# Linear-attention scan: levels paired by s and t+1, without a diagonal pass

## Chip, core and metric

One core of a Trainium2 chip runs one launch of the kernel. The metric is the device time of that launch in microseconds. The kernel before takes 2003.21 us in the median of three runs (2000.13 to 2006.03). The engines are named PE (matmuls), PEld (its weight loads), DVE (vector), ACT (scalar), POOL (GpSimd) and SP (which queues most transfers).

## The reference

The program is a stack of mixer and feed-forward parts on 512 tokens of width 1024, in fp32. The change lies in its first part, a linear attention with 8 heads of 128 features. Cut to that:

```
q = silu(q) * 128 ** -0.5
forget = lower_bound + (1 - lower_bound) * sigmoid(f)
k = 1 - forget
# per head, per chunk: cum = cumsum(log forget)
decay[t, s] = exp(cum[t] - cum[s])            # for s <= t, else 0; per feature
scores[t, s] = sum over features of q[t] * k[s] * decay[t, s]
o = scores @ v + (q * exp(cum)) @ state
state = exp(cum[last]) * state + (k * exp(cum[last] - cum)).T @ v
o = rms_norm(o, out_norm) * silu(g)           # then @ w_out
```

The decay of a pair (t, s) is the product of the forget values from s+1 to t, a vector over features, so it has to be put into q and k before the matmul over features.

## The kernel before, in words

All matmuls against weights are split in three: weights and activations are each a high and a low part of fp32r, and high x high, high x low and low x high are added (L329, L332, L333, three 128x512 matmuls a tile of 128x128 weights). ACT makes the high part of a chunk of 8 weight tiles (L1208), DVE the low one (L1887), both some chunks ahead.

**A head of the scan.** The 512 tokens are four blocks of 128, and q, k, the forget values (`ff`) lie with features on partitions and tokens along the row. Within a block the pairs (t, s) are sorted into the diagonal (s = t) and 7 levels. At level lv, spans of b = 2^lv tokens are taken in pairs: s lies in the first span, t in the second. The kernel walks the levels from 0 to 6. Before a level's scores, q in the second spans and k in the first ones have been multiplied step by step by the products of forget values that lie between (DVE: `qt`, L2040; POOL: `kt`, L2726), and POOL halves the row of forget products (`ft`, L2733, into `fb`). Each level is one pass of four matmuls, one a block (L441, `scores`; an fp32 matmul shows as two records in the trace), and one masked copy of the 128x512 result into `sc` (DVE, `pick`, L2022). The masks of the diagonal and the 7 levels come from `masks()` by a transfer at the start.

The diagonal's pass uses q itself (`a.q`, two buffers) before any product; the levels use `qa = q * ff` (L2009), one buffer. So `qa` waits until the output matmuls of the head before have read it. The passes use banks 3 and 4 in turn.

After the last level PE transposes k (L469), makes the states (L476) and the outputs (L487 with `sc`, L490 with `qa` and the state S); ACT takes the squares and the root (L1318, L1322), DVE scales (`og`, L2069), PE transposes `og` (L500), DVE applies gain and gate (L2075), and ACT and DVE split it into `ohi` (L1327) and `olo` (L2078), the operands of the output projection.

**The order.** Each engine runs its own program, written out by hand; semaphores named by head and level tie them (`sc_mm`: a pass is done; `qt`, `kt`, `ft`: the products; `cp`: the masked copy). `HG_TILES` says how many weight tiles of the next head's projections PE, ACT and DVE take after each step of a head's scan: none before the first pass, none between the diagonal and level 0, three behind level 0, two behind each later level. The last head's scan has the first tiles of the output projection there. An engine's instructions run in program order, so an instruction that waits holds all that stand behind it.

Of the kernel before, what the change touches and what calls it, by code (L numbers as in the profile page):

```python
# [9 lines left out]
I32 = mybir.dt.int32  # L10
# [5 lines left out]
T = 512  # L16
# [94 lines left out]
def memory(nc, ctx):  # L111
# [32 lines left out]
    with ExitStack() as ph:  # L144
        p = lambda name, shape, dt=F: sbt(ph, name, shape, dt)
        a = m.hg = Names()
        a.v = p("v", [128, 4, D])
        a.ohi = p("ohi", [128, KD, T], FR)
        a.olo = p("olo", [128, KD, T], FR)
        a.tq = p("tq", [128, 2, T])  # L150
        a.th = p("th", [128, 2, T])
        a.q = p("q", [128, 2, T])
        a.ff = p("ff", [128, 2, T])
        a.kk = p("kk", [128, 2, T])
        a.sg = p("sg", [128, 2, T])
        a.qa = p("qa", [128, T])
        a.fb = p("fb", [128, T])
        a.sc = p("sc", [128, 4, 128])
        a.kt = p("kt", [128, 3, 128])
        a.S = p("S", [128, 3, 128])  # L160
        a.og = p("og", [128, 2, T])
        a.mask = p("mask", [128, LV + 1, 128])
        a.ssq = p("ssq", [128, 2, 4])
        a.rch = p("rch", [128, 4])

# [111 lines left out]


HG_V_BANKS = [[0, 1, 2, 3], [4, 5, 6, 0]]
HG_TILES = [0, 0, 3, 2, 2, 2, 2, 2, 2, 2, 1, 1, 1, 3, 0, 1]  # L280
SWA_LEAD = 3
SWA_TILES = [4, 0, 1, 0, 0, 0, 1, 2, 0]
SWA_BEGUN = [0] * 6 + [1] * 7 + [0] + [2] * 7
# [36 lines left out]
def tensor_program(e, m, s):  # L320
# [82 lines left out]

    def hgrn():
        a = m.hg
        kk, qs, sc, S, v, qa = a.kk, a.q, a.sc, a.S, a.v, a.qa
        ready0 = operands_ready("n0")
        for g in range(2):
            for k in range(KD):
# [24 lines left out]
        def scan(h):  # L434
            z = h % 2
            hc = slice(128 * h, 128 * h + 128)

            def scores(level, b, qx):
                for c in range(4):
                    cs = slice(128 * c, 128 * c + 128)  # L440
                    op = e.matmul(B[b][:, cs], kk[:, z, cs], qx[:, cs], start=True, stop=True)  # L441
                op.then_inc(*s.sc_mm.tick(h, level))

            yield
            q.wait_ge(*s.made_v.at("k", h))
            if h:
                q.wait_ge(*s.made_a.at("kt", h - 1))
            else:
                q.wait_ge(*s.taken_a.at("v", 0, 3))
            scores(0, 3, qs[:, z, :])  # L450
            yield
            for lv in range(LV):
                if lv == 0:
                    q.wait_ge(*s.made_v.at("qa", h))
                    if h:
                        q.wait_ge(*s.made_v.at("S", h - 1, 2))
                    else:
                        q.wait_ge(*s.taken_a.at("v", 1, 0))
                else:
                    q.wait_ge(*s.qt.at(h, lv - 1))  # L460
                    q.wait_ge(*s.kt.at(h, lv - 1))
                    q.wait_ge(*s.cp.at(h, lv - 1))
                scores(lv + 1, 4 - lv % 2, qa)
                yield
            q.wait_ge(*s.kt.at(h, LV - 1))
            q.wait_ge(*s.cp.at(h, 6))
# [6 lines left out]
            q.wait_ge(*s.cp.at(h, 7))  # L473
            for c in range(3):
                cs = slice(128 * c, 128 * c + 128)
                op = e.matmul(B[4][:, cs], a.kt[:, c, :], v[:, c, hc], start=True, stop=True)  # L476
            op.then_inc(*s.valued.tick("S", h))
            yield
            bo = B[5 + z]
            if h > 1:  # L480
                q.wait_ge(*s.taken_v.at("o", h - 2))
            else:
                q.wait_ge(*s.taken_a.at("v", 1, 1 + h))
            q.wait_ge(*s.qt.at(h, LV - 1))
            for c in range(4):
                cs = slice(128 * c, 128 * c + 128)
                op = e.matmul(bo[:, cs], sc[:, c, :], v[:, c, hc], start=True, stop=c == 0)  # L487
                if c:
                    q.wait_ge(*s.made_v.at("S", h, c - 1))
                    op = e.matmul(bo[:, cs], qa[:, cs], S[:, c - 1, :], start=False, stop=True)  # L490
# [708 lines left out]
def scalar_program(e, m, s, A, chunks):  # L1199
# [69 lines left out]
    def hgrn():  # L1269
# [26 lines left out]
        def scan(h):  # L1296
            z = h % 2
            yield
            yield
# [580 lines left out]
def vector_program(e, m, s, chunks):  # L1880
# [94 lines left out]

    def hgrn():
        a = m.hg
        kk, ff, qs, sc, S, qa, th, tq, fb = a.kk, a.ff, a.q, a.sc, a.S, a.qa, a.th, a.tq, a.fb
        first_rows()
        root("n0", m.rc)  # L1980
        tables()
# [4 lines left out]
        def proj(h):  # L1986
# [19 lines left out]
            q.wait_ge(*s.made_v.at("q", h))  # L2006
            if h:
                q.wait_ge(*s.filled.at("o", h - 1))
            e.tensor_tensor(qa[:, :], qs[:, z, :], ff[:, z, :], MUL).then_inc(*s.made_v.tick("qa", h))  # L2009
            yield from w.steps(KD - 3)  # L2010

        def scan(h):
            z = h % 2

            def pick(level, b):
                q.wait_ge(*s.sc_mm.at(h, level))
                if level:
                    q.wait_ge(*s.cp.at(h, level - 1))
# [3 lines left out]
                e.copy_predicated(sc[:, :, :], a.mask[:, level, :].bitcast(I32).unsqueeze(1).to_broadcast((128, 4, 128)),  # L2022
                                  B[b].rearrange("p (c t) -> p c t", c=4)).then_inc(*s.cp.tick(h, level))

            yield
            pick(0, 3)
            yield
            fsrc = ff[:, z, :]
            for lv in range(LV):
                b = 1 << lv  # L2030
                n = T // (2 * b)
                fs = fsrc[:, 0:2 * n].rearrange("p (n a) -> p n a", a=2)
                qv = qa[:, :].rearrange("p (n a b) -> p n a b", a=2, b=b)
                q.wait_ge(*s.sc_mm.at(h, lv + 1))
                if lv:
                    q.wait_ge(*s.qt.at(h, lv - 1))
                    q.wait_ge(*s.ft.at(h, lv - 1))
                else:
                    q.wait_ge(*s.made_v.at("qa", h))
# [10 lines left out]
                o0 = 0 if lv % 2 == 0 else 256  # L2050
                fsrc = fb[:, o0:o0 + n]
                yield
            yield
            q.wait_ge(*s.valued.at("S", h))
# [655 lines left out]
def pool_program(e, m, s):  # L2710
    q = Waits(e)

    def hgrn(h):
# [3 lines left out]
        for lv in range(LV):  # L2717
# [4 lines left out]
            q.wait_ge(*s.sc_mm.at(h, lv + 1))  # L2722
            if lv:
                q.wait_ge(*s.kt.at(h, lv - 1))
                q.wait_ge(*s.ft.at(h, lv - 1))
            e.tensor_tensor(kv[:, :, 0, :], kv[:, :, 0, :], fs[:, :, 1:2].to_broadcast((128, n, b)),  # L2726
                            MUL).then_inc(*s.kt.tick(h, lv))
            fdst = a.fb[:, 256 * (lv % 2):256 * (lv % 2) + n]
            if h and lv == 0:
                q.wait_ge(*s.made_v.at("S", h - 1, 2))  # L2730
            if lv:
                q.wait_ge(*s.qt.at(h, lv - 1))
            e.tensor_tensor(fdst.unsqueeze(2), fs[:, :, 0:1], fs[:, :, 1:2], MUL).then_inc(*s.ft.tick(h, lv))  # L2733
            fsrc = fdst

    def sum_of_squares(site, i, width=T):
# [366 lines left out]
```

## Time and profile before

| what | value |
|---|---|
| median of three runs | 2003.21 us |
| lowest, highest | 2000.13, 2006.03 us |
| profiled execution | 2006.37 us |
| its span, first to last instruction | 2004.5 us |
| mean granted PE clock | 0.988 |
| PE, DVE, ACT, POOL busy | 97%, 69%, 42%, 11% |
| chain that ended last | PE 80%, DVE 12%, ACT 5%, issue 3% |

The profiled execution's own time is its span and some 2 us around it. Shares are means over stages with different limits; the scan takes about 220 of the 2004.5 us. Idle time of an engine counts only where another engine waits for it.

### The profile page before, as it was taken

How to read it: one execution, taken by the hardware profiler on the slowest of the kernel's cores; microseconds unless marked ns; L12 is line 12 of the kernel's file. 1: busy time of each engine (PE TensorE's matmuls, PEld its weight loads, DVE VectorE, ACT ScalarE, POOL GpSimd, SP SyncE). 2: the span in 40 equal slices, each digit the busy share in tenths (PEclk: the TensorE clock that was granted, in tenths of full speed). 3: DMA queues.
4: the chain of work that ended last, by engine and by line, in shares of the span. 5: the costliest groups of instructions: out<-in, count | busy, mean ns of one | idle time of the engine just before them, and what ended most of it. 6: DMA issues, size and time to landing. Idle time of an engine off the chain costs nothing.

```text
span 2004.5 us, 24575 instructions
## 1 busy us (share of the span) xinstructions
PE 1946.8 (97%) x9790; PEld 1632.7 (81%) x9790; DVE 1377.7 (69%) x1978; ACT 836.0 (42%) x1326; POOL 228.7 (11%) x233
## 2 busy tenths in 40 slices
PE   7999999999999999999999999999999999999997
PEld 6888887788888889888888888778888778888786
DVE  5477766997789578857755874555655477787774
ACT  5233334441233356644423443454444444454442
POOL 2133221003201230010000001000000101001011
PEclk9999999999999999999999999999999999999998
DMA  5211112335544431134343432311101323232321
GB/s 184 74 57 64 53 64 95 142 126 200 184 154 145 136 124 43 45 103 148 136 168 116 157 104 87 105 63 43 43 33 32 126 74 118 99 137 84 130 95 53
DMA packets 60818, 207.73 MB, mean 104 GB/s; under 512 B 6816, under 2 KB 7264, under 8 KB 59552
## 3 DMA queue, kind: packets, MB, share of 16 engines
q1 hardware_dynamic: 53152, 192.53, 28.3%
q10 hardware_dynamic: 7552, 13.64, 1.9%
q8 instruction: 77, 1.26, 0.3%
q14 instruction: 37, 0.30, 0.1%
HBM read 195.65 MB, written 10.49 MB: 103 GB/s over the span
## 4 chain that ended last, share of the span: by engine, by line
PE 80%; DVE 12%; ACT 5%; issue 3%; POOL 1%; DMA 1%; ACTq 0%; DVEq 0%; SPq 0%
PE PS L329 21%; PE PS L333 20%; PE PS L332 20%; PE PS L441 3%; DVE wlo L1887 2%; PE PS L945 2%; PE PS L336 1%; PE PS L339 1%; PE PS L340 1%; PE PS L737 1%; ACT whi L1208 1%; PE PS L934 1%; DVE col_f L2108 1%; PE PS L549 1%; PE PS L718 1%
## 5 line engine op out<-in xcount | busy, mean ns | idle before, releaser
L329 PE MATMUL PS<-nhi,whi 128*128 128x512 f32 x1456 | 589.7, 405 | 15.5 <-DVE wlo L1887 3.5
L333 PE MATMUL PS<-nhi,wlo 128*128 128x512 f32 x1456 | 572.4, 393 | 0.0
L332 PE MATMUL PS<-nlo,whi 128*128 128x512 f32 x1456 | 571.4, 392 | 0.0
L1887 DVE TENSOR_TENSOR wlo<-raw,whi 128x1024 fp32r<-128x1024 f32 x290 | 367.4, 1276 | 176.7 <-ACT whi L1208 175.5
L1208 ACT ACTIVATE whi<-raw 128x1024 fp32r<-128x1024 f32 x290 | 302.1, 1052 | 182.5 <-PE PS L329 112.4
L329 PEld LDWEIGHTS PS<-nhi,whi 128*128 128x128 f32 x1456 | 276.6, 190 | 77.4 <-issue 9.7
L333 PEld LDWEIGHTS PS<-nhi,wlo 128*128 128x128 f32 x1456 | 275.7, 189 | 60.1
L332 PEld LDWEIGHTS PS<-nlo,whi 128*128 128x128 f32 x1456 | 276.7, 190 | 52.2 <-issue 1.0
L2741 POOL TENSOR_TENSOR diag<-diag,sqb 128x512 f32<-128x512 f32 (+1 forms) x56 | 73.0, 1304 | 758.5 <-ACT sqb L1217 675.8
L329 PE MATMUL PS<-hh_f,whi 128*128 128x512 f32 x352 | 137.8, 392 | 0.0
L333 PE MATMUL PS<-hh_f,wlo 128*128 128x512 f32 x352 | 137.7, 391 | 0.0
L332 PE MATMUL PS<-hl_f,whi 128*128 128x512 f32 x352 | 137.5, 391 | 0.0
L2757 POOL TENSOR_TENSOR sd_f<-ab_f 128x512 f32<-128x512 f32 x32 | 55.3, 1745 | 271.6 <-DVE ab_f L2196 271.0
L2108 DVE SCALAR_TENSOR_TENSOR col_f<-aw_f,scv,col_f 128x1024 f32<-128x1024 f32 x63 | 85.0, 1359 | 0.0
L329 PEld LDWEIGHTS PS<-hh_f,whi 128*128 128x128 f32 x352 | 66.5, 189 | 13.9
L332 PEld LDWEIGHTS PS<-hl_f,whi 128*128 128x128 f32 x352 | 66.5, 189 | 13.8
L333 PEld LDWEIGHTS PS<-hh_f,wlo 128*128 128x128 f32 x352 | 66.3, 188 | 14.0
L1431 ACT ACTIVATE t_f<-gp_f,par 128x512 f32<-128x512 f32 x44 | 35.9, 816 | 94.3 <-DVE gp_f L2213 94.3
L1673 ACT ACTIVATE pt_m<-PS 128x768 f32<-128x768 f32 x32 | 26.0, 812 | 110.9 <-PE PS L934 110.9
L1931 DVE TENSOR_TENSOR hT<-hT,PS 128x512 f32<-128x512 f32 x48 | 32.7, 681 | 49.7 <-PE PS L333 49.6
L1907 DVE SCALAR_TENSOR_TENSOR nlo<-hT,par,nhi 128x512 fp32r<-128x512 f32 x32 | 38.9, 1222 | 37.4 <-ACT nhi L1230 37.4
L1217 ACT ACTIVATE sqb<-hT 128x512 f32<-128x512 f32 x42 | 26.5, 630 | 90.4 <-DVE hT L1931 57.9
(365 smaller groups left out, 3363.4 us busy)
## 6 DMA issues: line engine op xcount, KB each, us to landing
raw<-in_stream SPq DMA_DIRECT2D x290, 512.0 KB, 3.5
aw_f<-in_ada SPq DMA_DIRECT2D x48, 512.0 KB, 4.5
rows<-sd_f ACTq DMA_DIRECT2D x32, 256.0 KB, 2.3
rows_h<-rows SPq DMA_DIRECT2D x8, 1024.0 KB, 6.1
wd_f<-in_decay ACTq DMA_DIRECT2D x16, 256.0 KB, 2.9
hT<-in_xT SPq DMA_DIRECT2D x8, 256.0 KB, 7.5
out<-hT SPq DMA_DIRECT2D x8, 256.0 KB, 2.0
wd_f<-in_filt_out ACTq DMA_DIRECT2D x8, 128.0 KB, 2.9
```

The costliest lines, as they stand in the source:

```text
L329: op = e.matmul(out, hi, xh, start=first, stop=False)
L332: e.matmul(out, hi, xl, start=False, stop=False)
L333: return e.matmul(out, lo, xh, start=False, stop=last)
L441: op = e.matmul(B[b][:, cs], kk[:, z, cs], qx[:, cs], start=True, stop=True)
L945: op = e.matmul(B[6][:, 128 * blk:128 * blk + 128], a.v[:, t, 128 * h:128 * h + 128], a.pt[:, i, 128 * t:128 * t + 128], start=t == 0, sto ...
L1208: e.activation(m.whi[:, c % HL, :], m.raw[:, c % RAW, :], ACT.Copy).then_inc(*s.w_hi.tick(c))
L1431: e.activation(a.t[:, 0, z, :], a.gp[:, z, 2:T + 2], ACT.Identity, bias=pc(cb, f), scale=pc(cw, 44 + f)).then_inc(*s.made_a.tick("c0", lay ...
L1887: e.tensor_tensor(m.wlo[:, c % HL, :], m.raw[:, c % RAW, :], m.whi[:, c % HL, :].bitcast(F), SUB).then_inc(*s.w_lo.tick(c))
L1907: e.scalar_tensor_tensor(m.nlo[:, k, :], m.hT[:, k, :], gain, m.nhi[:, k, :].bitcast(F), MUL, SUB).then_inc(*s.nlo.tick(site, k))
L2108: e.scalar_tensor_tensor(col[:, v, :], aw[:, n % AW[layer], :], m.scv[:, 2, k, v:v + 1], col[:, v, :], MUL, ADD).then_inc(*s.made_v.tick(" ...
L2741: e.tensor_tensor(acc, acc, m.sqb[:, i % 2 if site != "n4" else 0, 0:width], ADD).then_inc(*s.acc.tick(site, i))
L2757: e.tensor_tensor(a.sd[:, x, :], a.ab[:, 0, :], a.ab[:, 1, :], SUB if x else ADD).then_inc(*s.made_p.tick("sd", n, i, x))
```

## The change

Levels are found from s and u = t + 1 in place of s and t. A pair with s = t then has s and u in neighbouring spans of some level, so the diagonal needs no pass. Pairs whose u is 128, the last token of a block, are in no level by this rule; the last token's q is kept in two extra columns of each block. Column HG_U + 128 is its running product, multiplied by forget products at level 5 and 6, and column HG_U + 129 the raw value, the diagonal of the last token.

So q lies in a row of four blocks of 160 columns, with u = 0 at column 15; `qa` and its product q * ff are gone, and the level products work on q in place. The last level scores 81 columns in place of 128, and two plain copies of parts of the block take the place of its masked copy. There are two masks fewer, and one step of the scan fewer in the order of PE, ACT and DVE, with its 0 in `HG_TILES`. POOL makes the forget product before the key product at level 5 alone. The writing of q waits for the output matmuls of two heads before.

```diff
-        a.q = p("q", [128, 2, T])
+        a.q = p("q", [128, 2, 4, 160])
-        a.qa = p("qa", [128, T])
-        a.mask = p("mask", [128, LV + 1, 128])
+        a.mask = p("mask", [128, LV - 1, 128])
...
-HG_TILES = [0, 0, 3, 2, 2, 2, 2, 2, 2, 2, 1, 1, 1, 3, 0, 1]
+HG_TILES = [0, 3, 2, 2, 2, 2, 2, 2, 2, 1, 1, 1, 3, 0, 1]
+HG_U = 15
+HG_LAST = 49
...
@@ tensor_program, scan @@
-            def scores(level, b, qx):
+            def scores(lv, b):
+                first = HG_LAST if lv == LV - 1 else 1
+                n = 130 - HG_LAST if lv == LV - 1 else 128
                 for c in range(4):
-                    op = e.matmul(B[b][:, cs], kk[:, z, cs], qx[:, cs], start=True, stop=True)
+                    op = e.matmul(B[b][:, 128 * c:128 * c + n], kk[:, z, 128 * c:128 * c + 128],
+                                  qs[:, z, c, HG_U + first:HG_U + first + n], start=True, stop=True)
...
-            q.wait_ge(*s.made_v.at("k", h))
-            if h:
-                q.wait_ge(*s.made_a.at("kt", h - 1))
-            else:
-                q.wait_ge(*s.taken_a.at("v", 0, 3))
-            scores(0, 3, qs[:, z, :])
-            yield
...
@@ vector_program, proj @@
-            e.scalar_tensor_tensor(qs[:, z, :], th[:, 0, :], 1.0, tq[:, 0, :], ADD, MUL).then_inc(*s.made_v.tick("q", h))
+            if h > 1:
+                q.wait_ge(*s.filled.at("o", h - 2))
+            last = lambda x: in_blocks(x)[:, :, 127:128]
+            e.scalar_tensor_tensor(qs[:, z, :, HG_U + 129:HG_U + 130], last(th[:, 0, :]), 1.0, last(tq[:, 0, :]), ADD,
+                                   MUL).then_inc(*s.made_v.tick("raw", h))
+            e.scalar_tensor_tensor(qs[:, z, :, HG_U + 1:HG_U + 129], in_blocks(th[:, 0, :]), 1.0, in_blocks(tq[:, 0, :]), ADD,
+                                   MUL).then_inc(*s.made_v.tick("q", h))
...
-            if h:
-                q.wait_ge(*s.filled.at("o", h - 1))
-            e.tensor_tensor(qa[:, :], qs[:, z, :], ff[:, z, :], MUL).then_inc(*s.made_v.tick("qa", h))
...
@@ vector_program, scan @@
+                if lv < LV - 1:
+                    op = e.copy_predicated(sc[:, :, :], a.mask[:, lv, :].bitcast(I32).unsqueeze(1).to_broadcast((128, 4, 128)), got)
+                else:
+                    e.tensor_copy(sc[0:64, :, 63:128], got[0:64, :, 64 - HG_LAST:129 - HG_LAST])
+                    op = e.tensor_copy(sc[64:128, :, 127:128], got[64:128, :, 129 - HG_LAST:130 - HG_LAST])
...
-                e.tensor_tensor(qv[:, :, 1, :], qv[:, :, 1, :], fs[:, :, 0:1].to_broadcast((128, n, b)),
-                                MUL).then_inc(*s.qt.tick(h, lv))
-                pick(lv + 1, 4 - lv % 2)
+                if lv < LV - 1:
+                    qv = qs[:, z, :, HG_U:HG_U + 128].rearrange("p c (n a b) -> p c n a b", a=2, b=b)[:, :, :, 1, :]
+                    op = e.tensor_tensor(qv, qv, fs[:, :, :, 0:1].to_broadcast((128, 4, n // 4, b)), MUL)
+                else:
+                    qv = qs[:, z, :, HG_U + 64:HG_U + 129]
+                    op = e.tensor_tensor(qv, qv, fs[:, :, 0, 0:1].to_broadcast((128, 4, 65)), MUL)
+                op.then_inc(*s.qt.tick(*((h, "row", lv) if lv == LV - 2 else (h, lv))))
...
+                if lv == LV - 2:
+                    x = qs[:, z, :, HG_U + 128:HG_U + 129]
+                    q.wait_ge(*s.ft.at(h, lv))
+                    e.tensor_tensor(x, x, in_blocks(fsrc)[:, :, 1:2], MUL).then_inc(*s.qt.tick(h, lv))
+                pick(lv, 4 - lv % 2)
...
@@ pool_program, hgrn @@
+            if lv == LV - 2:
+                forgets()
+                keys()
+            else:
+                keys()
+                forgets()
...
@@ masks @@
-    out = [s == t]
-    for lv in range(LV):
+    u = t + 1
+    out = []
+    for lv in range(LV - 1):
         b = 1 << lv
-        out.append((s // (2 * b) == t // (2 * b)) & (s // b % 2 == 0) & (t // b % 2 == 1))
+        out.append((s // (2 * b) == u // (2 * b)) & (s // b % 2 == 0) & (u // b % 2 == 1))
```

## Rows read from the trace of the kernel before

**Rows 1.** The page's busy times: busy us, share of the span, instructions.

```profile
PE 1946.8 (97%) x9790; PEld 1632.7 (81%) x9790; DVE 1377.7 (69%) x1978; ACT 836.0 (42%) x1326; POOL 228.7 (11%) x233
```

**Rows 2.** Windows, one head: PE, PEld, DVE, ACT, POOL busy (records), clock, DMA share, GB/s.

```profile
157.00:185.00 28.00, 27.56 (x166) 23.59 (x167) 20.23 (x34) 9.88 (x19) 8.67 (x14) 1.00 0.18 57
```

**Rows 3.** Groups by form, 75 to 297 us: busy us, mean ns, idle before.

```profile
L441 PE MATMUL PS<-qa,kk 128*128 128x128 f32 x448 | 60.1, 277 | 0.8
...
L2022 DVE COPY_PREDICATED sc<-mask,PS 128x512 f32<-128x512 int32 x64 | 47.7, 745 | 2.2 <-PE PS L441 2.2
...
L441 PE MATMUL PS<-q,kk 128*128 128x128 f32 x64 | 8.4, 274 | 0.0
...
L2009 DVE TENSOR_TENSOR qa<-q,ff 128x512 f32<-128x512 f32 x7 | 4.8, 693 | 1.4 <-PE PS L490 1.4
```

**Rows 4.** Chain of waits in order of time: start us, us, what.

```profile
158.31 1.78 PE PS L441 x16
...
162.18 0.89 PE PS L441 x8
...
454.06 3.46 PE PS L549 x32
```

**Rows 5.** Groups by form, 90 to 620 us: small operations on DVE.

```profile
L2055 DVE COPY S<-PS 128x128 f32<-128x128 f32 x8 | 2.3, 292 | 6.2 <-PE PS L476 6.2
...
L2065 DVE RECIPROCAL rch<-sd 128x4 f32<-128x4 f32 x8 | 1.4, 179 | 18.6 <-ACT sd L1322 18.6
```

**Rows 6.** Timeline: start of the fourth head's scan, DVE and POOL.

```profile
159.53 0.69 DVE L2078 TENSOR_TENSOR olo<-og,ohi 128x512 fp32r<-128x512 f32 x1 [0.69 <-ACT ohi L1327]
...
160.18 0.86 POOL L2726 TENSOR_TENSOR kk<-kk,ff 128x256 f32<-128x256 f32 x1 [11.92 <-PE PS L441]
...
160.80 0.52 DVE L2040 TENSOR_TENSOR qa<-qa,ff 128x256 f32<-128x256 f32 x1
...
160.99 0.80 POOL L2733 TENSOR_TENSOR fb<-ff 128x256 f32<-128x256 f32 x1
```

**Rows 7.** Timeline: the first head's level 0 on DVE.

```profile
77.00 0.43 DVE L2040 TENSOR_TENSOR qa<-qa,ff 128x256 f32<-128x256 f32 x1 [0.17 <-PE PS L441]
```

**Rows 8.** Timeline: levels 1 to 4 of the fourth head.

```profile
162.01 1.05 PE L441 MATMUL PS<-qa,kk 128*128 128x128 f32 x8
...
163.10 0.43 DVE L2040 TENSOR_TENSOR qa<-qa,fb 128x256 f32<-128x256 f32 x1 [0.55 <-PE PS L441]
...
163.15 1.00 POOL L2726 TENSOR_TENSOR kk<-kk,fb 128x256 f32<-128x256 f32 x1 [1.36 <-PE PS L441]
...
164.29 1.09 PE L441 MATMUL PS<-qa,kk 128*128 128x128 f32 x8
...
166.62 1.05 PE L441 MATMUL PS<-qa,kk 128*128 128x128 f32 x8
...
167.10 1.21 DVE L1887 TENSOR_TENSOR wlo<-raw,whi 128x1024 fp32r<-128x1024 f32 x1
...
167.75 1.06 POOL L2726 TENSOR_TENSOR kk<-kk,fb 128x256 f32<-128x256 f32 x1 [1.12 <-PE PS L441]
...
168.23 0.86 DVE L2040 TENSOR_TENSOR qa<-qa,fb 128x256 f32<-128x256 f32 x1
...
169.15 1.16 PE L441 MATMUL PS<-qa,kk 128*128 128x128 f32 x8
...
171.54 1.05 PE L441 MATMUL PS<-qa,kk 128*128 128x128 f32 x8
```

**Rows 9.** Timeline behind the scan: a POOL and a DVE operation together.

```profile
304.49 1.30 POOL L2741 TENSOR_TENSOR diag<-diag,sqb 128x512 f32<-128x512 f32 x1 [17.63 <-ACT sqb L1217]
...
305.06 1.28 DVE L1907 SCALAR_TENSOR_TENSOR nlo<-hT,par,nhi 128x512 fp32r<-128x512 f32 x1 [1.31 <-ACT nhi L1230]
```

**Rows 10.** Timeline: the fourth head's last level.

```profile
173.82 1.05 PE L441 MATMUL PS<-qa,kk 128*128 128x128 f32 x8
...
174.91 0.43 DVE L2040 TENSOR_TENSOR qa<-qa,fb 128x256 f32<-128x256 f32 x1 [0.62 <-PE PS L441]
```

More of the change, by code:

```diff
@@ L405, in hgrn @@
         a = m.hg
-        kk, qs, sc, S, v, qa = a.kk, a.q, a.sc, a.S, a.v, a.qa
+        kk, qs, sc, S, v = a.kk, a.q, a.sc, a.S, a.v
         ready0 = operands_ready("n0")
@@ L436, in scan @@
             hc = slice(128 * h, 128 * h + 128)
-            def scores(level, b, qx):
+            def scores(lv, b):
+                first = HG_LAST if lv == LV - 1 else 1
+                n = 130 - HG_LAST if lv == LV - 1 else 128
                 for c in range(4):
-                    cs = slice(128 * c, 128 * c + 128)
-                    op = e.matmul(B[b][:, cs], kk[:, z, cs], qx[:, cs], start=True, stop=True)
-                op.then_inc(*s.sc_mm.tick(h, level))
-            yield
-            q.wait_ge(*s.made_v.at("k", h))
-            if h:
-                q.wait_ge(*s.made_a.at("kt", h - 1))
-            else:
-                q.wait_ge(*s.taken_a.at("v", 0, 3))
-            scores(0, 3, qs[:, z, :])
+                    op = e.matmul(B[b][:, 128 * c:128 * c + n], kk[:, z, 128 * c:128 * c + 128],
+                                  qs[:, z, c, HG_U + first:HG_U + first + n], start=True, stop=True)
+                op.then_inc(*s.sc_mm.tick(h, lv))
             yield
@@ L453, in scan @@
                 if lv == 0:
-                    q.wait_ge(*s.made_v.at("qa", h))
+                    q.wait_ge(*s.made_v.at("q", h))
+                    q.wait_ge(*s.made_v.at("k", h))
                     if h:
@@ L461, in scan @@
                     q.wait_ge(*s.kt.at(h, lv - 1))
-                    q.wait_ge(*s.cp.at(h, lv - 1))
-                scores(lv + 1, 4 - lv % 2, qa)
+                    if lv > 1:
+                        q.wait_ge(*s.cp.at(h, lv - 2))
+                    elif h:
+                        q.wait_ge(*s.made_a.at("kt", h - 1))
+                    else:
+                        q.wait_ge(*s.taken_a.at("v", 0, 3))
+                scores(lv, 4 - lv % 2)
                 yield
             q.wait_ge(*s.kt.at(h, LV - 1))
-            q.wait_ge(*s.cp.at(h, 6))
+            q.wait_ge(*s.cp.at(h, LV - 2))
             for c in range(3):
@@ L472, in scan @@
             q.wait_ge(*s.made_a.at("kt", h))
-            q.wait_ge(*s.cp.at(h, 7))
+            q.wait_ge(*s.cp.at(h, LV - 1))
             for c in range(3):
@@ L489, in scan @@
                     q.wait_ge(*s.made_v.at("S", h, c - 1))
-                    op = e.matmul(bo[:, cs], qa[:, cs], S[:, c - 1, :], start=False, stop=True)
+                    op = e.matmul(bo[:, cs], qs[:, z, c, HG_U + 1:HG_U + 129], S[:, c - 1, :], start=False, stop=True)
             op.then_inc(*s.filled.tick("o", h))
@@ L1298, in scan @@
             yield
-            yield
             for lv in range(LV):
@@ L1977, in hgrn @@
         a = m.hg
-        kk, ff, qs, sc, S, qa, th, tq, fb = a.kk, a.ff, a.q, a.sc, a.S, a.qa, a.th, a.tq, a.fb
+        kk, ff, qs, sc, S, th, tq, fb = a.kk, a.ff, a.q, a.sc, a.S, a.th, a.tq, a.fb
         first_rows()
@@ L2005, in proj @@
             e.tensor_scalar(kk[:, z, :], ff[:, z, :], -1.0, 1.0, MUL, ADD).then_inc(*s.made_v.tick("k", h))
-            q.wait_ge(*s.made_v.at("q", h))
-            if h:
-                q.wait_ge(*s.filled.at("o", h - 1))
-            e.tensor_tensor(qa[:, :], qs[:, z, :], ff[:, z, :], MUL).then_inc(*s.made_v.tick("qa", h))
             yield from w.steps(KD - 3)
@@ L2013, in scan, with pick @@
             z = h % 2
[L2015 to L2018, printed above, removed]
+            def pick(lv, b):
+                got = in_blocks(B[b])
+                q.wait_ge(*s.sc_mm.at(h, lv))
+                if lv:
+                    q.wait_ge(*s.cp.at(h, lv - 1))
                 else:
@@ L2021, in pick @@
                     q.wait_ge(*s.setup_v.at("sc"))
[L2022 to L2026, printed above, removed]
+                if lv < LV - 1:
[3 more added lines that the diff above has]
+                    op = e.tensor_copy(sc[64:128, :, 127:128], got[64:128, :, 129 - HG_LAST:130 - HG_LAST])
+                op.then_inc(*s.cp.tick(h, lv))
             yield
@@ L2031, in scan @@
                 n = T // (2 * b)
-                fs = fsrc[:, 0:2 * n].rearrange("p (n a) -> p n a", a=2)
-                qv = qa[:, :].rearrange("p (n a b) -> p n a b", a=2, b=b)
-                q.wait_ge(*s.sc_mm.at(h, lv + 1))
+                fs = fsrc[:, 0:2 * n].rearrange("p (c n a) -> p c n a", c=4, a=2)
+                q.wait_ge(*s.sc_mm.at(h, lv))
                 if lv:
@@ L2038, in scan @@
                 else:
-                    q.wait_ge(*s.made_v.at("qa", h))
-                e.tensor_tensor(qv[:, :, 1, :], qv[:, :, 1, :], fs[:, :, 0:1].to_broadcast((128, n, b)),
-                                MUL).then_inc(*s.qt.tick(h, lv))
-                pick(lv + 1, 4 - lv % 2)
+                    q.wait_ge(*s.made_v.at("q", h))
+                if lv < LV - 1:
[5 more added lines that the diff above has]
+                op.then_inc(*s.qt.tick(*((h, "row", lv) if lv == LV - 2 else (h, lv))))
+                o0 = 0 if lv % 2 == 0 else 256
+                fsrc = fb[:, o0:o0 + n]
+                if lv == LV - 2:
[3 more added lines that the diff above has]
+                pick(lv, 4 - lv % 2)
                 if lv == 0:
@@ L2049, in scan @@
                                            MUL).then_inc(*s.made_v.tick("sg", h))
-                o0 = 0 if lv % 2 == 0 else 256
-                fsrc = fb[:, o0:o0 + n]
                 yield
@@ L2721, in hgrn, with keys, forgets @@
             kv = kx.rearrange("p (n a b) -> p n a b", a=2, b=b)
[L2722 to L2727, printed above, removed]
-            fdst = a.fb[:, 256 * (lv % 2):256 * (lv % 2) + n]
[L2729 to L2733, printed above, removed]
+            fdst = a.fb[:, 256 * (lv % 2):256 * (lv % 2) + n]
+            def keys():
+                q.wait_ge(*s.sc_mm.at(h, lv))
+                if lv:
+                    q.wait_ge(*s.kt.at(h, lv - 1))
+                    q.wait_ge(*s.ft.at(h, lv - 1))
+                e.tensor_tensor(kv[:, :, 0, :], kv[:, :, 0, :], fs[:, :, 1:2].to_broadcast((128, n, b)),
+                                MUL).then_inc(*s.kt.tick(h, lv))
+            def forgets():
+                if h and lv == 0:
+                    q.wait_ge(*s.made_v.at("S", h - 1, 2))
+                if lv:
+                    q.wait_ge(*s.qt.at(h, lv - 1))
+                    q.wait_ge(*s.ft.at(h, lv - 1))
+                e.tensor_tensor(fdst.unsqueeze(2), fs[:, :, 0:1], fs[:, :, 1:2], MUL).then_inc(*s.ft.tick(h, lv))
+            if lv == LV - 2:
+                forgets()
+                keys()
+            else:
+                keys()
+                forgets()
             fsrc = fdst
```

## Prediction

> **What bounds the kernel now.** I read the page's table of busy times first: PE is busy 97% of the span [rows 1]. Then the stage that the change touches, the eight heads of the scan (about 75 to 297 us), by windows: in the 28 us of one head PE is busy 27.6 us at a granted clock of 1.00, DVE 20.2, POOL 8.7 and the DMA engines 0.18 of the time [rows 2]. So PE sets the pace here, and work taken off DVE alone is worth nothing, unless PE was waiting for it. The groups by form price what goes and what stays [rows 3], the chain of waits gives PE's own pace [rows 4], and the timelines of one head show which operand comes last before each scoring pass [rows 6 to 8]. The head shown is the fourth; the ones after it repeat it.
>
> **PE: what is removed.** The diagonal pass is four fp32 matmuls, 8 records a head, 64 in all [rows 3]. In the chain the two adjoining passes take 1.78 us for 16 records and one pass 0.89 us for 8, so 0.111 us a record [rows 4]. Nothing else runs between them. The pass is worth 0.89 us a head, 8 x 0.89 = 7.1 us if nothing new comes last.
>
> The last level now scores 81 columns in place of 128. Nearest row: 32 records of one column each take 3.46 us, 0.108 us a record [rows 4], nearly the pace of 128 columns. That bounds the gain at 0.003 x 64 = 0.2 us; I take nothing. The Trainium skill (TensorE: Matmul & The Clock Gate, Back-to-back issue gap) gives columns/2.4 + 2.5 ns for an isolated matmul, by which a record of two such passes would fall by about 0.04 us and the 64 records by 2.5 us; the same section says that the formula leaves out the weight load, and the one-column row agrees with that.
>
> **DVE: what is removed and added, a head.** Gone: one masked copy (0.75) and the product q*f (0.69) [rows 3]. The last masked copy becomes two plain copies, of 64 x 260 and 64 x 4. A 128 x 128 copy from PSUM takes 0.29 us and a 128 x 512 masked copy 0.75 [rows 3, 5]; I take 0.43 for the first, and 0.18, as for a 128 x 4 reciprocal [rows 5], for the second, 0.61 together (at most 0.93 by the masked copy). Two operations on 128 x 4 come in, the raw last column and its product: 0.18 each, between nothing and 0.29 [rows 5]. Sum: 2.19 us gone, 0.97 added. DVE has idle time in the head, so this counts only where PE waits for DVE. The products on q now walk four blocks of 160 with the same number of elements; I take the same 0.43 to 0.52 us [rows 6, 8] and no cost, and keep +0.3 us as the upper bound (the data part again), nothing as the lower.
>
> **The start of a head: where a new wait arises.** Today two PE passes stand before the first products, so POOL begins its key product at 160.18, when DVE has just ended the low half of the previous head's output (olo, 159.53 for 0.69) [rows 6]. After the change the first pass is done at 160.09 - 0.89 = 159.20 [rows 4] and POOL starts at about 159.29, before DVE's olo. Both read two SBUF operands. What the trace shows when a POOL operation of that kind is under way and DVE starts such a one: DVE's ends 0.28 us (256 columns) or 0.55 us (512) after POOL's end, however early it began. So the level-3 product, 168.23 for 0.86 beside POOL's 167.75 to 168.81, ends 0.28 after it [rows 8]; the level-0 product, 160.80 for 0.52, ends 0.28 after POOL's 161.04 [rows 6]; a 512-column one at 305.06 takes 1.28 and ends 0.55 after POOL's 305.79 [rows 9]. Whoever waited longer comes next: at 168.31 POOL, waiting behind DVE's weight split, goes ahead of DVE's next product; at 161.04 the waiting DVE product goes ahead of POOL's next. The Trainium skill (SBUF — State Buffer, Who interferes with whom) states this as an exclusive lock on a shared port pair for a DVE instruction with two SBUF inputs against GpSimd; by that rule, the trace agrees.
>
> With these rows the start of the fourth head becomes:
> POOL keys 159.29 to 160.15 (0.86 alone [rows 6]).
> DVE olo from 159.53, held until 160.15, then 0.55: 160.70.
> POOL's forget product, there since 160.10, is next: its 0.47 after a release (today 161.32 to 161.79 [rows 6]): 161.17.
> DVE's level-0 product, there since 160.62: 161.17 + 0.28 = 161.45.
> PE wants the next pass at 162.01 - 0.89 = 161.12 [rows 8]. The product is 0.33 us late.
>
> What lateness costs: level passes that nothing delays start 2.28 us apart (162.01 to 164.29). From 166.62 to 171.54 two steps take 4.92 in place of 4.56, a loss of 0.36, where the level-3 product ended at 169.09, 0.19 after the due 168.90 [rows 8]. So a loss is lateness + 0.17, and 0.33 late costs 0.50 us. This holds for the seven heads with an olo before them. In the first head no olo stands before them, DVE is idle until the pass is done, and its product takes 0.43 [rows 7]: full 0.89.
>
> **Behind it.** The level-1 pass then starts at 161.51 and ends at about 162.67; DVE comes free of g's scaling just then. POOL's level-1 keys end at 163.76 whether DVE's product goes first (162.71 to 163.14, then 0.62 as today [rows 8]) or the DVE product follows (163.80); the pass is due at 161.51 + 2.28 + 0.11 = 163.90. Today the keys end at 164.15 against 164.29 [rows 8]: the same 0.14. Nothing more is lost there, and 0.1 at most. The wait at level 3 (0.36 us) hangs on the weight split behind the level-2 pass, moves with PE and stays. So does the wait for the output's norm at the head's end.
>
> Level 5: POOL makes the forget product first. It needs only level 4's, and POOL waits over a microsecond for each pass (1.36 us before 163.15 [rows 8]), so this fills idle time. DVE's product for the last column then meets POOL's keys and ends right behind them, at about 173.6 against a pass due at 173.82 [rows 10]. Cost nothing; if its 0.18 became 0.5, 0.1 a head. The masked copy and the q of the next head slip by 0.5 us; the level-6 product slips from 174.91 [rows 10] to about 175.6 and ends near 175.9, and is wanted only by the output matmuls, three steps later. The weight split behind it slips with it by some 0.4 us; its chunk is first used more than a chunk's matmuls later. The wait added before q is written, on the output of two heads before, ended a head earlier. Of transfers only the mask block changes, a quarter smaller, and no PE wait hangs on it.
>
> **Sum.** 8 x 0.89 = 7.1; 7 x 0.50 = 3.5 given back; 3.6 us gained. Against the profiled execution, 2006.4 us with a span of 2004.5, that is 2002.8; against the median of the runs, 2003.2, it is 1999.6 us, 0.18% less.
>
> **Rivals.**
> A. The port is not in the way, or DVE keeps it from olo to the product next to it: the product is done by 160.8 to 161.0, before 161.12. The full 7.1 us: 1996.1 us. For it: DVE takes back-to-back instructions with no gap. Against: at 168.31 DVE did lose the port between two of its own. Chance 0.20.
> B. My mechanism, with the block-wise product views, the extra column and the level-1 race each costing some 0.1 us: levels 0 and 3 pass all of it on, together about 0.27 us a head, 2.1 us: 2001.7 us. Chance 0.19.
> C. Slower. The products over four blocks of 160 run at half speed, +0.30 us each. Levels 0 and 3 lose it whole (0.60). POOL's keys wait behind the product: level 1 has 0.14 to spare and loses 0.16 + 0.17, level 2 has 0.25 and loses 0.22, levels 4 and 5 have 0.28 and lose 0.19 each. 1.53 a head, 12.2 in all, less 3.6: 2011.8 us. It turns the sign from about +0.2 us a product, where 0.45 us a head is lost. For it: no row shows DVE on such a view. Against: the products at span 1 and span 2 both take 0.43 undisturbed [rows 7, 8], whatever the step between their elements. Chance 0.07.
> The forecast itself: 0.54.
>
> **Numbers.** A measurement of this kernel can tell about 0.3%, 6.0 us (three runs lie from 2000.1 to 2006.0). The gain of 3.6 us is inside. Faster by over 0.3%: nearly all of A and a tenth of the forecast, 0.24. Slower: C and a little, 0.08. Within: 0.68. The range reaches to A's 1996.1 and a little below, and above B to where nothing is gained: 1995.5 to 2003.5; the forecast's own is 1998 to 2001.5.
>
> **What would show it.** The scoring group has 448 records, not 512; the head's period falls from 27.7 to about 27.3 us from the second head on, and the first by 0.9. Olo takes about 1.2 us in place of 0.69 in seven heads; the level-0 product about 0.8 in place of 0.52; and PE has a new wait for that product before the level-1 pass, seven times. The last-level pass keeps 0.11 us a record. If olo still takes 0.69, A is right; if the products take 0.7 us with POOL idle, C is. It would be wrong, too, if POOL's first keys started later than 159.3, or if a stage behind the scan lost or won time of its own.

## Result and the profile after

The changed kernel takes 1999.02 us in the median of ten runs (1996.57 to 2003.74); the kernel before, in ten, 2005.16 us (2000.13 to 2006.03). The ratio is 0.9977, 95% interval 0.9966 to 0.9988: 4.6 us less (2.4 to 6.8). The two medians lie 6.1 us apart and the two means 4.4 us (2003.7 and 1999.2): of the ten times of the kernel before, three lie at 2000.1 to 2000.5 and seven at 2003.2 to 2006.0, so its median moves easily. The forecast was 3.6 us less and 1999.6 us.

The page of the changed kernel:

```profile
span 1997.5 us, 24456 instructions
...
PE 1938.4 (97%) x9726; PEld 1622.5 (81%) x9726; DVE 1376.4 (69%) x1986; ACT 836.1 (42%) x1326; POOL 231.2 (12%) x233
```

PE has 9726 records, 64 fewer than in [rows 1]. The same 28 us of the fourth head, by windows (the columns as in [rows 2]):

```profile
155.00:183.00 28.00, 27.31 (x160) 23.02 (x161) 20.60 (x35) 9.88 (x19) 9.01 (x14) 1.00 0.19 57
```

The 28 us hold a little more than one head, so for DVE whole heads are the better measure: over the seven from the first to the last transposes of the scaled output it is busy 136.5 us, and in the kernel before 136.4. The work taken off it comes back as four small operations and as time that others spend held. The groups by form show where (busy us, mean ns, idle before):

```profile
L443 PE MATMUL PS<-q,kk 128*128 128x128 f32 x384 | 52.4, 279 | 2.4 <-DVE q L2047 1.5
...
L443 PE MATMUL PS<-q,kk 128*128 128x81 f32 x64 | 8.1, 269 | 0.0
...
L2752 POOL TENSOR_TENSOR fb<-ff 128x256 f32<-128x256 f32 x8 | 8.1, 1006 | 0.0
...
L2092 DVE TENSOR_TENSOR olo<-og,ohi 128x512 fp32r<-128x512 f32 x7 | 8.0, 1149 | 4.9 <-ACT ohi L1328 4.9
...
L2047 DVE TENSOR_TENSOR q<-q,ff 128x256 f32<-128x256 f32 x8 | 6.2, 780 | 2.8 <-PE PS L443 2.8
```

The diagonal's pass is gone (384 + 64 records, where [rows 3] had 448 + 64). Olo (L2092) has a mean of 1.15 us and the level-0 product (L2047 on `ff`) 0.78. Of the new operations the copies from PSUM take 0.41 and 0.17 us, the last level's product 0.43, the raw column 0.15, the last column's product 0.58. The start of the fourth head on the timeline:

```profile
156.21 1.05 PE L443 MATMUL PS<-q,kk 128*128 128x128 f32 x8
...
157.34 0.86 POOL L2743 TENSOR_TENSOR kk<-kk,ff 128x256 f32<-128x256 f32 x1 [11.08 <-PE PS L443]
...
157.59 1.16 DVE L2092 TENSOR_TENSOR olo<-og,ohi 128x512 fp32r<-128x512 f32 x1 [0.70 <-ACT ohi L1328]
...
158.16 1.06 POOL L2752 TENSOR_TENSOR fb<-ff 128x256 f32<-128x256 f32 x1
...
158.67 0.83 DVE L2047 TENSOR_TENSOR q<-q,ff 128x256 f32<-128x256 f32 x1
...
159.56 1.16 PE L443 MATMUL PS<-q,kk 128*128 128x128 f32 x8 [0.21 <-DVE q L2047]
...
160.80 1.00 POOL L2743 TENSOR_TENSOR kk<-kk,fb 128x256 f32<-128x256 f32 x1 [1.58 <-PE PS L443]
...
161.94 1.09 PE L443 MATMUL PS<-q,kk 128*128 128x128 f32 x8
```

The reader should follow the ends. POOL's keys end at 158.20. Olo, under way since 157.59, ends at 158.75, 0.55 later. POOL's forget product, there since 158.16, ends at 159.22, 0.47 later. DVE's level-0 product, there since 158.67, ends at 159.50, 0.28 later. PE was due for the next pass at 159.18, 2.97 us after the first (in the kernel before they are 3.86 apart, 158.15 and 162.01, with the 0.89 us of the removed pass in between), and begins it at 159.56. On the chain of waits this stretch, which was PE's alone in the kernel before [rows 4], now reads:

```profile
157.59 1.16 DVE olo L2092
158.75 0.77 DVE q L2047
...
159.56 1.16 PE PS L443 x8
```

And among the waits of the stage (us, times, longest) stands one that was not there, seven of the fifteen in the first row (the other eight are level 3's) and all of the last:

```profile
PEld PS L443 <- DVE q L2047: 8.8, 15, 0.6
...
PE PS L443 <- DVE q L2047: 1.5, 7, 0.2
```

**Period of a head.** The transposes of the scaled output (L500, in the changed kernel L502) mark each head. The table takes the first and the last of the eight from each timeline, and a seventh of their distance. These periods repeat within 0.06 us from head to head, where whole runs of one kernel differ by 5 us and more.

| kernel | first, last transposes (us) | period | ratio to before, 95% |
|---|---|---|---|
| before | 101.52, 295.58 | 27.72 | |
| changed | 100.39, 291.59 | 27.31 | 0.9977 (0.9966 to 0.9988) |
| e1_olo_late | 101.56, 289.28 | 26.82 | 0.9964 (0.9952 to 0.9977) |
| e2_before_olo_late | 100.54, 294.52 | 27.71 | 0.9996 (0.9985 to 1.0007) |
| e3_olo_one_sbuf | 100.84, 288.94 | 26.87 | 0.9955 (0.9941 to 0.9968) |
| e4_last_128 | 100.13, 291.34 | 27.32 | 0.9980 (0.9971 to 0.9989) |
| e5_keys_first | 101.35, 294.21 | 27.55 | 0.9993 (0.9984 to 1.0002) |
| e6_gate_early | 99.82, 288.32 | 26.93 | 0.9966 (0.9952 to 0.9979) |
| e7_olo_late_gate_early | 99.68, 284.72 | 26.43 | 0.9948 (0.9935 to 0.9962) |
| e8_norm_cover | 100.00, 281.23 | 25.89 | 0.9926 (0.9912 to 0.9940) |
| e9_before_three_moves | 101.31, 288.61 | 26.76 | 0.9960 (0.9946 to 0.9973) |
| e10_all_again | 100.52, 281.60 | 25.87 | 0.9925 (0.9911 to 0.9938) |

In the first head the way from the first pass to the transposes falls from 26.51 us (75.01 to 101.52) to 25.61 (74.78 to 100.39), by 0.90. The scan as a whole, first pass to last transposes, falls from 220.57 to 216.81 us, by 3.76.

### The profile page after: what moved, and what is told of

Same layout as the page of the kernel before. It is cut to its first block, busy times and chain, and to the rows that moved or that the text cites. A ratio compares the mean times of both kernels' runs of the same rounds, so it can differ in the third digit from the quotient of the medians.

```text
span 1997.5 us, 24456 instructions
## 1 busy us (share of the span) xinstructions
PE 1938.4 (97%) x9726; PEld 1622.5 (81%) x9726; DVE 1376.4 (69%) x1986; ACT 836.1 (42%) x1326; POOL 231.2 (12%) x233
## 4 chain that ended last, share of the span: by engine, by line
PE 78%; DVE 13%; ACT 5%; issue 3%; POOL 1%; DMA 0%; ACTq 0%; DVEq 0%; SPq 0%
PE PS L330 20%; PE PS L334 20%; PE PS L333 20%; DVE wlo L1888 3%; PE PS L443 2%; PE PS L947 2%; ACT whi L1210 1%; PE PS L337 1%; PE PS L341 1%; PE PS L340 1%; PE PS L739 1%; PE PS L936 1%; DVE col_f L2122 1%; DVE q L2047 1%; PE PS L551 1%
## 5 line engine op out<-in xcount | busy, mean ns | idle before, releaser
L443 PEld LDWEIGHTS PS<-q,kk 128*128 128x128 f32 x448 | 56.6, 191 | 13.3 <-DVE q L2047 8.8
```

The source lines that it names most:

```text
L443: op = e.matmul(B[b][:, 128 * c:128 * c + n], kk[:, z, 128 * c:128 * c + 128], qs[:, z, c, HG_U + first:HG_U + first + n], start=True, sto ...
```

## The experiments

The theory: a removed pass is worth 0.89 us; in seven heads olo, which reads two SBUF operands, now starts behind POOL's first key product, is held by it, and so makes the level-0 product too late for PE. Each kernel has the change unless said otherwise.

**1. Olo behind the work of level 0.**

```diff
+        def low_part(h):
+            q.wait_ge(*s.hid_hi.at("o", h))
+            e.tensor_tensor(a.olo[:, h, :], ...).then_inc(*s.hid_lo.tick("o", h))
...
@@ level 0, behind the scaling of g @@
+                    if h:
+                        low_part(h - 1)
...
-            q.wait_ge(*s.hid_hi.at("o", h))
-            e.tensor_tensor(a.olo[:, h, :], ...).then_inc(*s.hid_lo.tick("o", h))
+            if h == KD - 1:
+                low_part(h)
```

> The changed kernel, but DVE makes the low half of the previous head's output (olo) behind level 0's product, masked copy and scaling of g, no longer before them; only the order on DVE changes. Theory (olo and POOL's first key product want the same port, and the level-0 product comes out 0.3 us late for PE): olo back to 0.69 us, the level-0 product starts right behind the first pass and takes 0.43 us, no PE wait before the level-1 pass, 0.5 us less a head in the seven later heads, so the scan is 3.3 to 3.5 us shorter than in the changed kernel and the time 7 to 8 us below the kernel before. Rival 1 (PE waits for something else there, for instance POOL's first keys): the wait before the level-1 pass stays, time as the changed kernel. Rival 2 (the gain of a removed pass never was 0.89 us a head): no wait, but the heads stay at 27.3 us.

The timeline of the same head:

```profile
156.37 1.05 PE L443 MATMUL PS<-q,kk 128*128 128x128 f32 x8
...
157.46 0.43 DVE L2051 TENSOR_TENSOR q<-q,ff 128x256 f32<-128x256 f32 x1 [0.40 <-PE PS L443]
...
157.51 1.11 POOL L2749 TENSOR_TENSOR kk<-kk,ff 128x256 f32<-128x256 f32 x1 [11.07 <-PE PS L443]
...
159.04 0.70 DVE L2017 TENSOR_TENSOR olo<-og,ohi 128x512 fp32r<-128x512 f32 x1
...
159.35 1.05 PE L443 MATMUL PS<-q,kk 128*128 128x128 f32 x8
```

The level-0 product takes 0.43 us right behind the pass, olo 0.70 later on, and PE begins the next pass on time, 2.98 us after the first (3.35 in the changed kernel). The waits on products have shrunk to the eight of level 3:

```profile
PEld PS L502 <- DVE og L2089: 6.1, 8, 0.8
...
PEld PS L443 <- DVE q L2051: 4.3, 8, 0.5
```

The period is 26.82 us: 0.49 less than changed, 0.90 less than before, and the scan is 3.47 us shorter than in the changed kernel (213.34 against 216.81). Rivals 1 and 2 fall by the periods and the waits. The whole runs can't tell the two kernels apart: their medians are 0.9 us apart, and the intervals of the ratios overlap. Part of it can be followed in the profiled executions: this one is 3.9 us ahead at a group of 16 matmul records far behind the scan (1174.04 against 1177.93) and only 1.1 us ahead at a pair of matmuls later on (1593.93 against 1595.02), with PE's granted clock lower in between (last section).

**2. The same move in the kernel before.**

> The kernel before, with the same move of olo behind level 0's work. Theory: there PE has two passes in front of the products, the product is 0.7 us early with olo in front, so the move gives nothing: heads at 27.73 us, time within 0.5 us of the kernel before. Rival (olo's place alone is worth what the first experiment shows, whatever the diagonal's pass): 3 us or more below the kernel before.

27.71 us against 27.72, ratio 0.9996 (0.9985 to 1.0007). The interval of the whole runs reaches from 3.0 us less to 1.4 more, too wide for the 0.5 us that was expected; the period decides. Olo's place was worth nothing there; it became worth something by the change.

**3. Olo with one SBUF operand.** Same place, same size; in seven heads it subtracts from the transposed output in PSUM, which leaves out the right low half.

```diff
-            e.tensor_tensor(a.olo[:, h, :], a.og[:, 1, :], a.ohi[:, h, :].bitcast(F), SUB)
+            e.tensor_tensor(a.olo[:, h, :], stat if h < KD - 1 else a.og[:, 1, :], a.ohi[:, h, :].bitcast(F), SUB)
```

> The changed kernel in its own order, but in the first seven heads olo takes its first operand from PSUM (the transposed output before gain and gate) in place of SBUF; same size, same place, only one SBUF operand; this leaves out the right low half of these heads. Theory (it is the second SBUF operand that makes DVE wait for POOL): olo 0.69 us although POOL's key product runs beside it; POOL's forget product then runs at once behind the keys, the level-0 product ends about 0.28 us behind it, at 0.1 us before PE is due: no wait or under 0.1 us, 2.8 to 3.4 us below the changed kernel. Rival (DVE is slowed by any POOL operation beside it, or olo is simply in the way by its place): olo 1.16 us still and PE's wait stays, time as the changed kernel.

```profile
156.93 0.86 POOL L2743 TENSOR_TENSOR kk<-kk,ff 128x256 f32<-128x256 f32 x1 [11.07 <-PE PS L443]
...
157.18 0.69 DVE L2092 TENSOR_TENSOR olo<-PS,ohi 128x512 fp32r<-128x512 f32 x1 [0.70 <-ACT ohi L1328]
...
157.74 0.62 POOL L2752 TENSOR_TENSOR fb<-ff 128x256 f32<-128x256 f32 x1
...
157.79 0.85 DVE L2047 TENSOR_TENSOR q<-q,ff 128x256 f32<-128x256 f32 x1
...
158.76 1.09 PE L443 MATMUL PS<-q,kk 128*128 128x128 f32 x8
```

Olo starts while POOL's keys run (156.93 to 157.79), as in the changed kernel, and takes 0.69 us. The forget product follows the keys at once; the level-0 product, which has two SBUF operands still, is held until 158.36 and ends 0.28 later, at 158.64. PE's pass starts at 158.76, on time, with 1.09 us. The period is 26.87, 0.44 less than changed. So it is olo's second SBUF operand, and not its place or POOL's mere activity. The 0.05 us above the first experiment are this pass's: its weight load starts at 158.69, 0.07 in front of it, where an undisturbed one starts 0.16 to 0.23 in front, and the next pass comes 2.32 us later (161.08) in place of 2.27 in the first experiment.

**4. The last level with 128 columns.**

```diff
-HG_LAST = 49
+HG_LAST = 2
```

> The changed kernel with the last level scoring 128 columns again (columns 2 to 129 of each block) in place of 81. Theory (a record's pace is set by its weight load): the pass of 8 records keeps 0.89 us, heads unchanged within 0.03 us, time as the changed kernel. Rival (a record is priced by its columns): 0.3 us more a head, 2.5 us above the changed kernel.

27.32 us against 27.31, ratio 0.9980 against 0.9977: 81 columns cost what 128 do.

**5. POOL's old order at level 5.**

```diff
-            if lv == LV - 2:
-                forgets()
-                keys()
-            else:
-                keys()
-                forgets()
+            keys()
+            forgets()
```

> The changed kernel with POOL's old order at level 5: the key product first, the forget product behind it. Theory (DVE's product of the last column needs level 5's forget product, and the next pass needs that column): the forget product ends about 0.2 us behind the keys, the column's product 0.15 us later, at some 0.1 us past the time at which PE is due for the last pass; with 0.17 us for a late start that is 0.2 to 0.3 us a head, heads at 27.5 to 27.6 us, about 2 us above the changed kernel, and a new PE wait on the column's product, eight times. Rival (the last pass has slack enough, the order is worth nothing): heads at 27.31 us.

```profile
171.76 0.86 POOL L2743 TENSOR_TENSOR kk<-kk,fb 128x256 f32<-128x256 f32 x1 [1.23 <-PE PS L443]
...
172.59 0.20 POOL L2752 TENSOR_TENSOR fb<-fb 128x8 f32<-128x8 f32 x1
...
172.82 0.17 DVE L2057 TENSOR_TENSOR q<-q,fb 128x4 f32<-128x4 f32 x1 [0.68 <-POOL fb L2752]
...
173.04 1.12 PE L443 MATMUL PS<-q,kk 128*128 128x81 f32 x8
```

The keys end at 172.62, the forget product at 172.79, the column's product at 172.99; PE was due at 172.90 (the last tile's first matmul at 172.21 and three of 0.23) and starts at 173.04. 27.55 us, 0.24 a head more, 1.9 us over eight heads; the ratio to before goes from 0.9977 to 0.9993, with intervals that overlap. A 0.20 us operation in the wrong place costs half of what the change gives.

**6. The gate one level earlier.**

```diff
-                elif lv == 2:
+                elif lv == 1:
                     q.wait_ge(*s.made_a.at("tg", h))
```

> The changed kernel, but DVE makes the gate of g (0.78 us) behind level 1's masked copy, where it stands idle for 1.2 us, in place of level 2's; then the weight split behind level 2 starts 0.7 us earlier and DVE is free when the level-3 product comes up. Theory (the wait before the level-4 pass is DVE's queue, and costs lateness + 0.17 us): the wait goes, 0.36 us a head, heads at 26.95 us, 2.9 us below the changed kernel. Rival (the wait comes from POOL's keys of level 3, behind the weight split's port): it shrinks but stays, under 0.15 us a head.

The timeline from level 1 on:

```profile
160.39 0.68 DVE L2064 SCALAR_TENSOR_TENSOR sg<-th,tq 128x512 f32<-128x512 f32 x1
...
162.69 1.33 DVE L1888 TENSOR_TENSOR wlo<-raw,whi 128x1024 fp32r<-128x1024 f32 x1
...
164.00 0.42 DVE L2047 TENSOR_TENSOR q<-q,fb 128x256 f32<-128x256 f32 x1
...
165.18 1.05 PE L443 MATMUL PS<-q,kk 128*128 128x128 f32 x8
```

The gate (160.39) stands behind level 1's copy. The weight split (162.69) begins 0.96 us after the level-2 product's start instead of 1.68, the level-3 product (164.00) takes 0.42 us in place of 0.87, and the pass behind it comes 2.27 us after the one before it (162.91). Period 26.93, 0.38 less than changed. The wait is gone and not only shorter, so POOL's keys were not what held PE there.

**7. Both moves.**

> The changed kernel with both moves, olo behind level 0's work and the gate behind level 1's. Theory (two waits in different places): they add up, heads at 26.82 - 0.36 = 26.46 us, the time 10 us below the kernel before. Rival (one takes the room of the other: DVE is full at level 1): heads at 26.6 to 26.8 us.

26.43 us: 0.88 less than changed, where the two alone gave 0.49 and 0.38. They add up.

**8. More cover for the norm.** Both moves, and the head's last tile in front of the transposes:

```diff
-HG_TILES = [0, 3, 2, 2, 2, 2, 2, 2, 2, 1, 1, 1, 3, 0, 1]
+HG_TILES = [0, 3, 2, 2, 2, 2, 2, 2, 2, 1, 1, 1, 4, 0, 0]
```

> As the run before it in this call (both moves), and PE, ACT and DVE take the head's last weight tile in front of the transposes of the scaled output instead of behind them, so that 0.69 us more of matmuls cover the norm's chain. Theory (PE waits there 0.35 us by the trace and loses 0.56 us to the pace, whatever the diagonal's pass): the wait goes, heads at 25.9 to 26.0 us, the time 14 us below the kernel before. Rival (the first pass now follows the transposes at once, and its products are late instead): a wait before the level-1 pass, heads at 26.3 us or more.

25.89 us. What PE still waits for in the scan:

```profile
PEld PS L443 <- issue: 1.6, 8, 0.2
...
PEld PS L330 <- DVE olo L2017: 0.2, 1, 0.2
```

Nothing on DVE's products and nothing on the norm; the move in front of the transposes gave 0.54 us a head. What is left are the eight waits marked issue. They are the weight load of the level-1 pass, and they stand in the kernel before and in the changed one with the same 1.6 us; what PE is short of there is said below, at level 1. The ratio is 0.9926, 14.8 us less than the kernel before, and its interval (0.9912 to 0.9940) lies below that of the changed kernel too. It beats both kernels.

**9. The three moves without the change.**

> The kernel before, with its diagonal pass, and the three moves of the last run (olo behind level 0's work, the gate behind level 1's, the last weight tile in front of the transposes). Theory (the moves take away waits that the kernel before has too, 0.36 and 0.56 us a head, and olo's place is worth nothing there): heads at 27.71 - 0.92 = 26.8 us, so that against the last run, at 25.89, the diagonal's pass is worth its full 0.89 us a head once nothing comes late; the time 6.5 to 7.5 us below the kernel before. Rival (the moves only work in the changed kernel): heads at 27.2 us or more.

26.76 us, ratio 0.9960 (0.9946 to 0.9973). The moves are worth 0.96 us a head there, and the scan is 6.98 us shorter (213.59 against 220.57); by the ratio it is 8.0 us (5.4 to 10.8), where 6.5 to 7.5 were expected; against the eighth run, at 25.89, the diagonal's pass is worth 0.87 us a head.

**10. The eighth run once more.**

> The kernel with the change and all three moves once more, beside the run before it on the same chip. Theory: heads at 25.89 us again, the time 7 us below that run and 14 us below the kernel before; what stages behind the scan add or take away by PE's granted clock differs from run to run by some us in either kernel.

25.87 us, 0.89 below the ninth; ratio 0.9925 (0.9911 to 0.9938). Against the ninth on the same chip the medians are 1989.87 and 1996.79 us, 6.9 less.

## Why the prediction held

**The pass: 0.89 us a head.** Right. The first head, which has no olo in front, lost 0.90. With olo moved the others lost 0.90 (experiment 1), and with no wait at all 0.87 to 0.89 (experiments 8 and 10 against 9).

**The last pass at 81 columns: nothing.** Right: 0.01 us a head (experiment 4). The formula by columns alone would have given 0.3 us a head.

**The start of a head.** Right step by step. Forecast, from the first pass's end: keys 0.86, olo held to 0.55 behind them, the forget product 0.47 behind olo, the level-0 product 0.28 behind that. Measured: 0.86, 0.55, 0.47, 0.28. The product was to be 0.33 us late and was 0.32. That the second SBUF operand does it was argued from [rows 6, 8, 9] and is shown by experiment 3. The Trainium skill (SBUF — State Buffer, Who interferes with whom) says that a DVE instruction with at most one SBUF input, outside the two-port modes, does not contend with GpSimd; olo's 0.69 us beside the keys in experiment 3 agrees. The order of grants, the longer waiting one first, is what both timelines have; no experiment tried it by itself.

**What lateness costs: lateness + 0.17.** 0.50 forecast, 0.49 found by taking the wait away. The level-3 wait, put at 0.36, gave 0.38 when removed (experiment 6), and the one made at level 5 fits too: 0.09 late, 0.24 lost (experiment 5).

**Level 1 with the margin of today.** Right that nothing changes, wrong that 0.14 us is a margin. The keys end at 161.80, 0.14 before the pass, as before; DVE's product went first, by 0.05 us. But the keys are what the weight load reads, and that is due earlier than the pass:

```profile
161.87 0.97 PEld L443 LDWEIGHTS PS<-q,kk 128*128 128x128 f32 x8 [0.20 <-issue]
...
161.94 1.09 PE L443 MATMUL PS<-q,kk 128*128 128x128 f32 x8
...
164.26 1.05 PE L443 MATMUL PS<-q,kk 128*128 128x128 f32 x8
```

The weight load starts 0.07 behind the keys' end and 0.07 in front of the pass, the pass lasts 1.09 us, and the next one comes 2.32 later; without a delay it is 2.28. Both kernels have this (164.22, 164.29 and 166.62 in the one before), and so has every run here. That POOL's keys cause it is read from the times; the profile names no releaser, and no experiment took it away. It costs 0.04 to 0.05 us a head in either kernel, so the forecast difference is untouched.

**Level 5.** Right that it costs nothing as written, and right in how (the fourth head):

```profile
170.32 0.86 POOL L2743 TENSOR_TENSOR kk<-kk,fb 128x256 f32<-128x256 f32 x1 [0.88 <-PE PS L443]
...
170.62 0.58 DVE L2057 TENSOR_TENSOR q<-q,fb 128x4 f32<-128x4 f32 x1
...
171.47 1.01 PE L443 MATMUL PS<-q,kk 128*128 128x81 f32 x8
```

The column's product takes 0.58 us, mostly waiting, and ends 0.02 behind POOL's keys, 0.27 before the pass. Alone it takes 0.17 (experiment 5). One size was off: the level-6 product was to end near 175.9, 2.1 us after its pass began (173.82); it ends at 172.95, 1.5 us after 171.47, since DVE came free just ahead of POOL's keys and was not held. Nothing hung on that.

**The new products' view.** No dearer: 0.43 us undisturbed, as in [rows 7, 8]. Rival C falls with that. So does B: neither the views, nor the extra column, nor level 1 cost more than before.

**Sum.** 7 x 0.41 + 0.90 = 3.8 us in the scan, forecast 3.6. The whole runs say 4.6 (2.4 to 6.8), which holds both. That the median came out at 1999.02, within 0.6 us of the forecast 1999.6, is luck: the forecast started from the 2003.21 us of three runs, and ten runs gave 2005.16. The two profiled spans differ by 7.0 us; 4.2 of them are there by the 16-record group at 1182.13 in the one and 1177.93 in the other, 2.9 more arise between it and the pair of matmuls at 1602.10 and 1595.02, where nothing was changed (last section). Rival A fell with olo's 1.15 us; its 0.89 us for every head is what experiment 1 has, with another order on DVE.

## What to carry to other kernels

A pass taken out in front of a two-engine step also takes away a head start. Go through who now starts first, and whether both read two SBUF operands: here the DVE operation that started second ended 0.28 us (256 columns) or 0.55 us (512 columns) after POOL's, and the product behind it came 0.32 us too late for PE. Then move the instruction nobody waits for, here olo: its place costs nothing before the change and 3.4 us after it.

A stretch where PE is 98% busy can hold more in waits than a removed pass gives: two short ones that the change did not touch, at level 3 and at the norm, were worth 0.96 us a head together, against 0.89.

## What the runs showed of the hardware

**A late operand costs more than its lateness, and one that is just in time costs too.** Three waits show 0.15 to 0.19 us on top of the lateness: the weight load, which undisturbed starts 0.16 to 0.23 us in front of its pass, starts within 0.01 us of it (159.55 and 159.56), and the pass lasts 1.16 us in place of 1.05 (1.12 in place of 1.01 with 81 columns). An operand that ends 0.12 to 0.14 us before the pass leaves the weight load 0.07 us and costs 0.04 to 0.05 (level 1, and level 0 in experiment 3). Where the keys ended 0.22 us before the pass (experiment 6, 162.69 and 162.91), the next pass came 2.27 us later and nothing was lost. So look at PEld's start and not only at PE's.

**A masked copy isn't held by POOL.** Its mask is in SBUF and its data are in PSUM: 0.75 us (161.09) beside POOL's keys (160.80 to 161.80), as in its groups (0.74 us on average).

**PE's granted clock falls in short stretches that come and go from run to run.** They go with the 5 to 6 us by which runs of one kernel differ: among 20 runs of the kernel before beside experiments 1 to 4, the one that took 1999.4 us has a mean clock of 0.991 and the one that took 2005.95 has 0.988. By windows (columns as in [rows 2]), a later part of the profiled kernel before:

```profile
1256.00:1260.00 4.00, 3.36 (x31) 3.19 (x29) 2.15 (x2) 2.93 (x4) 1.28 (x1) 1.00 0.46 153
1260.00:1264.00 4.00, 4.00 (x20) 3.75 (x19) 0.89 (x2) 1.48 (x3) 0.00 (x0) 0.57 0.35 131
1292.00:1296.00 4.00, 4.00 (x15) 3.16 (x14) 0.90 (x1) 0.00 (x0) 0.00 (x0) 0.73 0.43 134
```

PE stood idle for 0.64 us and then ran at a granted clock of 0.57 for 4 us, most of it at 1.2 in place of 2.4 GHz, and again at 0.73 some 32 us on, there behind 2.6 us of idling. The same work in experiment 3, where the stretch begins 8 us earlier:

```profile
1248.00:1252.00 4.00, 3.36 (x30) 3.19 (x29) 2.04 (x2) 2.77 (x5) 1.28 (x1) 1.00 0.49 154
1252.00:1256.00 4.00, 4.00 (x31) 3.52 (x30) 2.30 (x5) 1.82 (x4) 0.00 (x0) 1.00 0.31 121
1276.00:1280.00 4.00, 1.37 (x5) 0.53 (x4) 0.95 (x2) 2.96 (x6) 0.73 (x1) 1.00 0.06 26
```

The same idle time of 0.64 us, and a longer one of 2.63, and the clock stays at 1.00. From the 16-record group in front (1182.13 and 1173.80) to a pair of matmuls behind (1602.10 and 1589.30) the one takes 420.0 us and the other 415.5. The profiled changed kernel takes 417.1 (1177.93 to 1595.02): it has the first fall (0.57 from 1256 to 1260), but neither the second nor the third, which the kernel before has from 1540 to 1544 (0.58). My estimate from these clocks: 4 us at 0.57 lose 1.7 us, and the three falls of the kernel before some 5 us. None of this follows the change: experiment 4, with the change, takes 419.9 us (1177.78 to 1597.72), and experiment 1 the same (1174.04 to 1593.93). Why the clock falls in one run and not in the other stays open.
